# Two transformer blocks with product-key experts: expert picks in waves of 32 tokens, the convolution interleaved with the gathers

## The chip, the core and the metric

The program runs on one core of a Trainium2 chip, in fp32, for one sequence of 256 tokens of width 1024. The metric is the device time of one execution in microseconds. Before the change it is 2983.41 us, the median of 3 runs (2981.97 to 2993.83).

## The reference, cut to what matters

The first block has two layers. Each ends in an expert layer: per token and head, 16 experts of 16384 are chosen by product keys, and each chosen expert contributes one row of a table u (a dot product with the token) and one row of a table v (added with a weight). The mixer between the two expert layers is a convolution of 31 taps, so a token needs its neighbours 15 to either side. Then a second block of two layers (feed-forward, mixer, feed-forward) follows, which the change doesn't touch.

```python
s = jnp.einsum("thpd,hpnd->thpn", q, sub_keys)            # q = hb @ w_query, 8 heads, 2 halves
s_top, i_top = lax.top_k(s, 16)
cand = (s_top[:, :, 0, :, None] + s_top[:, :, 1, None, :]).reshape(...)
best, pos = lax.top_k(cand, 16)
expert = jnp.take_along_axis(cand_idx, pos, axis=-1)      # cand_idx = i_top[0] * 128 + i_top[1]
gate = jax.nn.softmax(best, axis=-1)
act = gelu(einsum("thkd,td->thk", jnp.take(u_tab, expert, axis=0), hb))
y = einsum("thk,thkd->td", gate * act, jnp.take(v_tab, expert, axis=0))
# a layer: h += g1 * mixer(modulate(rms_norm(h)));  h += g2 * experts(modulate(rms_norm(h)))
# mixer of layer 0: attention; of layer 1: conv = pw2(silu(layer_norm(depthwise31(glu(pw1(a))))))

```

## The kernel before

All five engines run programs written out in order; semaphores join them. Weights come as tiles of 512 KB (128 partitions of 1024 fp32 values), loaded by the sync engine SP in the order of the plan into four slots; SP refills a slot when TensorE (PE) has done with it. A tile is multiplied by `linear`: 8 matmuls, each recorded as two MATMUL rows, since an fp32 matmul leaves two records.

The phases are `ada`, `attn`, `peer` 0, `conv`, `peer` 1 and then the second block. An expert layer (`peer`) has 256 picks: head by head, for each of two blocks of 128 tokens, 16 picks. A pick `k` is one expert for each of 128 tokens:

- GpSimd (POOL) issues one indirect DMA (line 830) that fetches 128 rows of u and v together, 8 KB per token, 1.05 MB in all, into slot `k % PAIR_RING` of a ring of 14 slots. It waits until PE has used the slot's former content (`v_used`), and, every 16 picks, until VectorE (DVE) has chosen the experts (`expert_ready`).
- DVE makes the 128 dot products (line 2365), ScalarE (ACT) the gelu (1138), DVE multiplies by the gate (2372, `weigh`), ACT spreads the 128 weights on the diagonal of a 128x128 matrix (1145), and PE multiplies that by the rows of v in two matmuls of 512 columns (1742), which add up in two banks of PSUM per token block.

A choice (`choose`, lines 2309 to 2349) turns key scores of one head and 128 tokens into 16 experts. It stands on DVE two choices ahead of its use. Queries and scores of later heads are computed by PE between picks. The last four picks of a layer are summed by DVE. Then the sums are turned back, and the residual is updated for all tokens (`back`).

`conv` runs between the two expert layers, with no gather in flight: RMS norm, 16 tiles for `pw1` with a gate (ACT sigmoid 1188, DVE 2436), 31 taps per channel chunk (six chunks on DVE, line 2454; two on PE with diagonal matrices made by ACT, 1099), layer norm, `pw2`. The 14 last rows of the modulation weights (`rest_of_rows`, line 797) are loaded in it and reduced by DVE (2075). The first expert layer's `attn_w_out` product for the second token block runs inside `peer` 0 (`late`), as that of `pw2` does inside `peer` 1. After `peer` 1, `h_res` is turned to token-major (1793) and the feed-forward starts with row norms (ACT 922) and its first matmul (1679).

## Time and profile before

| | |
|---|---|
| median of 3 runs | 2983.41 us |
| span of the profiled execution | 2988.1 us |
| PE, DVE, ACT, POOL busy over the span | 87%, 65%, 37%, 21% |
| DMA | 832.42 MB, mean 279 GB/s |
| gathers (indirect DMAs) | 512 |
| weight tiles | 453 |

The profiled execution's own time is its span; nothing else of it is given. The page divides the span into 40 slices of 74.7 us. Its DMA row reads, in tenths of busy share and in GB/s:

```
DMA  9940899999999734999999998555425555542454
GB/s 299 391 163 1 300 419 420 420 420 420 421 420 420 304 99 140 420 417 420 420 420 420 420 420 355 183 183 168 156 67 183 183 161 184 183 161 75 150 188 148
```

So the 16 DMA engines are full in two long stretches, the expert layers, and nearly idle in the attention before them and in the convolution between them. "Busy" of an engine is the time in which an instruction of it is running; "idle before" names what ended a wait.

### The profile page before, as it was taken

The numbers are of one execution on the slowest core, as the hardware profiler recorded it, in microseconds if no ns is written. First come the engines' busy times: TensorE is split into PE (matmuls) and PEld (weight loads), VectorE is DVE, ScalarE is ACT, GpSimd is POOL, SyncE is SP. The second block draws the span as 40 slices with busy tenths as digits, with TensorE's granted clock in tenths as the row PEclk, the third lists the DMA queues.
The fourth block names the chain that finished last, engine by engine and source line by source line (L and its number), as shares of the span: only waits on it lengthen the run. The fifth ranks groups of instructions, "written<-read, shape, count | busy, mean of one in ns | idle before, by whom it ended". The sixth has DMA issues, their size and how long they took to land. (4 is left out here: it accounts for less than half of the span.)

```text
span 2988.1 us, 36198 instructions
## 1 busy us (share of the span) xinstructions
PE 2612.3 (87%) x11546; PEld 1723.9 (58%) x11546; DVE 1952.1 (65%) x4771; ACT 1112.4 (37%) x2639; POOL 633.9 (21%) x600
## 2 busy tenths in 40 slices
PE   7989888888777797898887787899989999999998
PEld 3534744333232387543333332898849989985798
DVE  1866476777676496686677765666746666675565
ACT  3245332222222312332222222445544454464544
POOL 0410245444444100354443542000000000000000
PEclk9989999999989898999999999899999999999999
DMA  9940899999999734999999998555425555542454
GB/s 299 391 163 1 300 419 420 420 420 420 421 420 420 304 99 140 420 417 420 420 420 420 420 420 355 183 183 168 156 67 183 183 161 184 183 161 75 150 188 148
DMA packets 152951, 832.42 MB, mean 279 GB/s; under 512 B 17008, under 2 KB 17136, under 8 KB 86384
## 3 DMA queue, kind: packets, MB, share of 16 engines
q0 software_dynamic: 85392, 579.38, 47.0%
q1 hardware_dynamic: 65664, 238.65, 24.1%
q10 hardware_dynamic: 1760, 12.70, 1.3%
q8 instruction: 71, 1.16, 0.2%
q14 instruction: 64, 0.52, 0.0%
HBM read 829.61 MB, written 1.05 MB: 278 GB/s over the span
## 5 line engine op out<-in xcount | busy, mean ns | idle before, releaser
L1742 PE MATMUL ps<-arena 128*128 128x512 f32 x1440 | 683.3, 619 | 162.4 <-ACT arena L1145 162.2
L2365 DVE SCALAR_TENSOR_TENSOR arena<-arena 128x1024 f32<-128x1024 f32 x368 | 450.1, 1224 | 227.4 <-DMA arena<-experts,arena 227.3
L1742 PEld LDWEIGHTS ps<-arena 128*128 128x128 f32 x1440 | 268.3, 195 | 562.8 <-ACT arena L1145 292.1
L830 POOL DMA_INDIRECT arena<-experts,arena x368 | 413.1, 1123 | 847.4 <-PE ps L1742 487.4
L2101 DVE TENSOR_TENSOR w_lo<-weights,w_hi 128x512 fp32r<-128x512 f32 x528 | 364.3, 691 | 280.7 <-ACT w_hi L910 278.8
L1145 ACT ACTIVATE arena<-con,arena 128x128 f32<-128x128 f32 x504 | 203.0, 403 | 730.1 <-DVE arena L2372 730.1
L910 ACT ACTIVATE w_hi<-weights 128x512 fp32r<-128x512 f32 x528 | 332.9, 632 | 375.4 <-PE ps L1681 278.8
L1679 PE MATMUL ps<-a_hi,w_hi 128*128 128x256 f32 x1408 | 399.8, 284 | 5.8 <-DVEq L2120 2.7
L1681 PE MATMUL ps<-a_hi,w_lo 128*128 128x256 f32 x1408 | 398.9, 283 | 0.0
L1680 PE MATMUL ps<-a_lo,w_hi 128*128 128x256 f32 x1408 | 398.9, 283 | 0.0
L1742 PE MATMUL ps<-held,arena 128*128 128x512 f32 x576 | 277.8, 625 | 79.6 <-ACT arena L1145 79.6
L1679 PEld LDWEIGHTS ps<-a_hi,w_hi 128*128 128x128 f32 x1408 | 270.5, 192 | 10.6 <-DVEq L2120 3.1
L1680 PEld LDWEIGHTS ps<-a_lo,w_hi 128*128 128x128 f32 x1408 | 270.5, 192 | 3.1
L1681 PEld LDWEIGHTS ps<-a_hi,w_lo 128*128 128x128 f32 x1408 | 270.4, 192 | 0.0
L1742 PEld LDWEIGHTS ps<-held,arena 128*128 128x128 f32 x576 | 109.8, 199 | 244.6 <-ACT arena L1145 131.9
L2365 DVE SCALAR_TENSOR_TENSOR held<-held,arena 128x1024 f32<-128x1024 f32 x144 | 175.9, 1222 | 83.5 <-DMA held<-experts,arena 83.5
L1435 PE MATMUL ps<-sq,weights 128*128 128x256 f32 (+1 forms) x1088 | 209.9, 355 | 17.9 <-ACT sq L904 12.3
L1435 PEld LDWEIGHTS ps<-sq,weights 128*128 128x128 f32 x1088 | 186.7, 201 | 44.3 <-issue 20.0
L830 POOL DMA_INDIRECT held<-experts,arena x144 | 163.8, 1138 | 199.1 <-PE ps L1742 184.4
L1011 ACT ACTIVATE arena<-ps 128x256 f32<-128x256 f32 (+5 forms) x182 | 83.4, 463 | 229.0 <-PE ps L1435 132.3
L1690 PE MATMUL ps<-w_hi,v_hi 128*128 128x512 f32 x352 | 138.6, 394 | 4.7 <-DVE v_lo L2521 4.7
L1690 PE MATMUL ps<-w_hi,v_lo 128*128 128x512 f32 x352 | 138.1, 392 | 0.0
(279 smaller groups left out, 3508.4 us busy)
## 6 DMA issues: line engine op xcount, KB each, us to landing
weights<-stream SPq DMA_DIRECT2D x453, 512.0 KB, 3.4
arena<-mod_rows_in POOLq DMA_DIRECT2D x71, 512.0 KB, 9.1
arena<-experts,arena POOLq DMA_INDIRECT x368, 25.8
mod_rows<-mod_rows_in POOLq DMA_DIRECT2D x9, 512.0 KB, 8.7
arena<-gain_rows ACTq DMA_DIRECT2D x1, 3072.0 KB, 11.5
held<-experts,arena POOLq DMA_INDIRECT x144, 26.1
arena<-rpb_windows ACTq DMA_DIRECT2D x4, 512.0 KB, 16.5
arena<-keys_in ACTq DMA_DIRECT2D x2, 1024.0 KB, 6.6
```

The source lines that it names most:

```text
L830: pool.indirect_dma_start(out=pair_of(k), out_offset=None, in_=experts[l], in_offset=bass.IndirectOffsetOnAxis(ap=expert[:, k:k + 1], axis ...
L910: act.activation(w_hi[:, o % 2, part], weights[:, t.unit, part], ACT.Copy).then_inc(hi_ready, 1)
L1011: taken(act.activation(dst, src, ACT.Copy), pr)
L1145: act.activation(diag[:, k % DIAGS, :], const("ident"), ACT.Copy, scale=act_w[:, k:k + 1]).then_inc(diag_ready, 1)
L1435: ins = pe.matmul(dst, wt(t, k, a, b), rhs(k), start=(k == 0), stop=(k == KC - 1))
L1679: pe.matmul(dst, w_hi[:, o % 2, cut], a_hi[:, k, :], start=(k == 0), stop=False)
L1680: pe.matmul(dst, w_hi[:, o % 2, cut], a_lo[:, k, :], start=False, stop=False)
L1681: ins = pe.matmul(dst, w_lo[:, o % 2, cut], a_hi[:, k, :], start=False, stop=(k == KC - 1))
L1690: ins = pe.matmul(ps[:, 2 * tb + half, :], v[:, b, at], w[:, o % 2, cut], start=(start and n == 0), stop=False, skip_group_check=True)
L1742: ins = pe.matmul(ps[:, 2 * b + half, :], diag[:, k % DIAGS, :], v_of(k, HALF * half, HALF * (half + 1)), start=(k == TOPK * b), stop=(k = ...
L2101: dve.tensor_tensor(w_lo[:, o % 2, part], weights[:, t.unit, part], w_hi[:, o % 2, part].bitcast(F32), ALU.subtract) \
L2365: dve.scalar_tensor_tensor(out=u, in0=u, scalar=1.0, in1=h_rows[:, b, :], op0=ALU.mult, op1=ALU.mult, accum_out=act_raw[:, k:k + 1]).then_ ...
```

## The change

The two expert layers and the convolution become one phase, `gather`, of 512 picks ("beats"). Every engine's program is generated from one table, `gather_order`: at each beat an engine does its part of pick `k` and then the steps that the table lists for it.

- A pick now serves 32 tokens and four heads (4 x 32 = 128 partitions) instead of 128 tokens and one head. Eight waves of 32 tokens per layer, two groups of heads per wave, 16 picks per group: 256 picks per layer, as before, and 32 choices in all, as before. Scores are computed per group, 32 rows at a time (`scores`), and the token rows are repeated four times (`rows`).
- A wave is finished after 32 picks. The diagonal matrix has 32 columns (`token`, 128x32), and the two matmuls of a pick write two of four column groups of the array (32 output partitions each, even picks groups 0 and 1, odd picks 2 and 3) in one bank. After each wave the sums are copied, added and turned by four small matmuls (`fold`), and DVE updates 32 columns of the residual in 8 operations.
- The gate is multiplied on ACT (a Copy with a scale) instead of on DVE. All 512 picks go through PE; the DVE sum of the last four is gone.
- The convolution runs in two blocks beside the gathers, block 0 from beat 130 and block 1 from beat 258: gates for 128 columns each, outputs for 96 and 160. Four channel chunks are tapped on PE (was two), four on DVE (was six). Queries of the second expert layer follow each block (96 and 160 columns), and `pw2` is whole per block.
- As each matrix is now used for two blocks of tokens, its tiles are loaded twice: 32 query tiles per layer (was 18), 32 for `pw1` (was 16), 16 for `pw2` (was 16 with the late half), 8 `late` tiles in layer 0: 120 tiles (was 76).
- The 14 modulation rows are loaded one by one between gathers of layer 0, into two slots.
- The ring of gathered pairs has 10 slots instead of 14 (`ARENA_PAIRS` 6 instead of 10, plus 4). The buffers of the convolution take the room.
- A choice stands on DVE at beat 16(c - 1) + 1, one group ahead; the first choice waits for the queries of four heads (8 tiles) where it waited for one head (2 tiles).

The core of the diff:

```diff
-PEER_BANKS = [4, 5, 6]
-TURN_BANK = 7
...
+FOLD_BANK, SCORE_BANK, TAP_BANK = 2, 3, 7
+WORK_BANKS = [4, 5, 6]
...
-TAPPED = [6, 7]
-EARLY_TAPS = 16
-ARENA_PAIRS = 10
...
+WAVE = 32
+WAVES = T // WAVE
+GROUP_HEADS = P // WAVE
+WAVE_GROUPS = H // GROUP_HEADS
+GROUPS = WAVES * WAVE_GROUPS
+WAVE_PICKS = WAVE_GROUPS * TOPK
+PICKS = GROUPS * TOPK
+GLU_COLS = [slice(0, 128), slice(128, 256)]
+OUT_COLS = [slice(0, 96), slice(96, 256)]
+WIDEST = 160
+PW1_ORDER = [4, 0, 1, 5, 2, 3, 6, 7]
+TAPPED = [4, 5, 6, 7]
+DIRECT = [(0, 1), (2, 3)]
+TAP_PART = 4
+TAP_DIAGS = 8
+ARENA_PAIRS = 6
 PAIR_RING = ARENA_PAIRS + 4
-TAP_ROWS = 8
...
+    for m in range(2 * H):
+        put("query", 0, 0, m, pe=-1, act=-1)
+        if m % (2 * GROUP_HEADS) == 2 * GROUP_HEADS - 1:
+            c = m // (2 * GROUP_HEADS)
+            put("scores", c, pe=-1, act=-1)
+            put("choose", c, dve=c - 1)
+            if c == 0:
+                put("rows", 0, pe=-1, act=-1)
...
+    for m in range(KC):
+        put("late", m, pe=1 + m, dve=6 + 5 * (m // 4))
+    put("late_squares", 0, act=12)
+    put("late_norm", 0, pe=13, act=14, dve=15)
+    put("shift_late", 0, act=16)
+    for m in range(2 * H):
+        put("query", 0, 1, m, pe=20 + 4 * m, act=21 + 4 * m)
+    for k in range(LATE_ROWS):
+        put("late_row", k, pool=16 + 6 * k, dve=20 + 6 * k)
...
+    for b, base in enumerate((130, 258)):
+        put("conv_squares", b, act=base + 1)
+        put("conv_sum", b, pe=base + 2, act=base + 3, dve=base + 4)
+        put("conv_shift", b, act=base + 5)
+        for i, c in enumerate(PW1_ORDER):
+            put("pw1", b, c, pe=base + 6 + 3 * i, act=base + 8 + 3 * i, dve=base + 9 + 3 * i)
+        for n, pair in enumerate(DIRECT):
+            first = base + (16, 25)[n]
+            for part in range(0, TAPS, TAP_PART):
+                put("direct", b, n, part, dve=first + part // TAP_PART)
+        parts = -(-TAPS // TAP_PART)
+        for n, c in enumerate(TAPPED):
+            for part in range(parts):
+                beat = base + 11 + parts * n + part
+                put("diags", b, c, part, act=beat)
+                put("taps", b, c, part, pe=beat + 1)
+            put("tap_out", b, c, act=base + 11 + parts * (n + 1) + 1)
+        last = base + 12 + parts * len(TAPPED)
+        put("mean", b, pe=last + 1, dve=last + 2)
+        put("var", b, act=last + 3, pe=last + 4)
+        put("var_root", b, act=last + 5)
+        put("spread", b, dve=last + 6, act=last + 7)
+        for m in range(KC):
+            put("pw2", b, m, pe=last + 8 + m, dve=last + 10 + m)
+        put("next_squares", b, act=last + 19)
+        put("next_sum", b, pe=last + 20, act=last + 21, dve=last + 22)
+        put("next_shift", b, act=last + 23)
+        for m in range(2 * H):
+            beat = last + 24 + (2 * m if b == 0 else m if m < H else m + 2)
+            put("query", 1, b, m, pe=beat, act=beat + 1)
+    put("new_keys", 0, act=222)
+    for c in range(2, ALL_GROUPS):
+        beat = TOPK * (c - 1)
+        late = 3 if c == GROUPS + WAVE_GROUPS * 3 else 0
+        put("scores", c, pe=beat - 6 + late, act=beat - 4 + late)
+        put("choose", c, dve=beat + 1)
+        put("exps", c, act=beat + 6)
+    for v in range(ALL_WAVES):
+        if v:
+            put("rows", v, pe=WAVE_PICKS * v - 12, act=WAVE_PICKS * v - 10)
+        end = WAVE_PICKS * (v + 1)
+        put("fold", v, act=end, pe=end + 1, dve=end + 2)
+    return order
+
+
+ORDER = gather_order()
+FIRST_BEAT, END_BEAT = -1, ALL_PICKS + 3
+TILED_STEPS = {"query": 1, "pw1": 2, "pw2": 1}
+
...
+            def late_row(k):
+                pool.wait_ge(row_dot, EARLY_ROWS if k < 2 else EARLY_ROWS + k - 1)
+                pool.dma_start(late_slots[k % 2], mod_rows_in[EARLY_ROWS + k]).then_inc(late_landed[k % 2], 16)
...
-                        pool.wait_ge(expert_ready, CHOICES * l + k // TOPK + 1)
-                    if base + k >= PAIR_RING:
-                        pool.wait_ge(v_used, base + k - PAIR_RING + 1)
-                    if l == 0 and k == LATE_SLOT:
-                        last = PL["peer", l]["t_late"][KC - 1]
-                        pool.wait_ge(tile_done[last.unit], last.first)
+                        pool.wait_ge(expert_ready, k // TOPK + 1)
+                    if k >= PAIR_RING:
+                        pool.wait_ge(v_used, k - PAIR_RING + 1)
...
+                    act.wait_ge(dot_done, k + 1)
+                    act.activation(act_out[:, one], act_raw[:, one], ACT.Gelu).then_inc(gelu_done, 1)
+                    if k % TOPK == 0:
+                        act.wait_ge(gate_set, k // TOPK + 1)
+                    act.wait_ge(gelu_done, k + 1)
+                    act.activation(act_w[:, one], act_out[:, one], ACT.Copy, scale=gate[:, one]).then_inc(weighed, 1)
+                    act.wait_ge(weighed, k + 1)
+                    if k >= DIAGS:
+                        act.wait_ge(v_used, k - DIAGS + 1)
+                    act.activation(diag[:, k % DIAGS, :], const("token"), ACT.Copy, scale=act_w[:, one]) \
+                        .then_inc(diag_ready, 1)
...
+                    pe.wait_ge(diag_ready, k + 1)
+                    pe.wait_ge(pair_landed[k % PAIR_RING], landed(k))
+                    for half in range(2):
+                        first = WAVE * (2 * (k % 2) + half)
+                        ins = pe.matmul(ps[first:first + WAVE, v % 2, :], diag[:, k % DIAGS, :],
+                                        v_of(k, HALF * half, HALF * (half + 1)), start=(k % WAVE_PICKS < 2),
+                                        stop=(k % WAVE_PICKS >= WAVE_PICKS - 2), skip_group_check=True)
+                    ins.then_inc(v_used, 1)
...
+                        for h in range(GROUP_HEADS):
+                            m = 2 * (first + h) + e
+                            ins = pe.matmul(bank(pr)[WAVE * h:WAVE * (h + 1), NKEY * e:NKEY * (e + 1)],
+                                            pq[:, m, WAVE * wave:WAVE * (wave + 1)], sub_keys[:, m, :],
+                                            start=True, stop=True, skip_group_check=True)
...
+                def fold(v):
+                    pr = pl["fold", v]
+                    pe.wait_ge(y_copied, v + 1)
...
+                    for c in range(4):
+                        ins = pe.matmul(bank(pr)[:, 2 * WAVE * c:2 * WAVE * (c + 1)], y_wave[:, P * c:P * (c + 1)],
+                                        const("halves"), start=True, stop=True)
...
+                    if k % WAVE_PICKS == 0:
+                        wait_taken(dve, pl["rows", v][1])
+                    u = u_of(k)
+                    dve.wait_ge(pair_landed[k % PAIR_RING], landed(k))
+                    dve.scalar_tensor_tensor(out=u, in0=u, scalar=1.0, in1=h_rows[:, v % 2, :], op0=ALU.mult,
+                                             op1=ALU.mult, accum_out=act_raw[:, at:at + 1]).then_inc(dot_done, 1)
```

## Rows read from the trace of the kernel before

**Rows 1.** Busy time by stretch; columns on the first row.
```profile
core 0: us, PE busy (x) PEld busy (x) DVE busy (x) ACT busy (x) POOL busy (x), PEclk, DMA share, GB/s
340.00:1010.00 670.00, 544.56 (x1373) 249.83 (x1371) 464.85 (x1379) 189.39 (x612) 285.75 (x254) 0.95 1.01 416
1013.00:1187.00 174.00, 142.31 (x709) 125.42 (x710) 127.93 (x320) 46.89 (x117) 7.39 (x14) 0.86 0.40 134
```

**Rows 2.** Timeline: one pick in the steady state.
```profile
1846.34 1.23 DVE L2365 SCALAR_TENSOR_TENSOR held<-held,arena 128x1024 f32<-128x1024 f32 x1 [1.17 <-DMA held<-experts,arena]
1847.68 0.40 ACT L1145 ACTIVATE arena<-con,arena 128x128 f32<-128x128 f32 x1 [1.98 <-DVE arena L2372]
1847.98 0.19 ACT L1138 ACTIVATE arena<-arena 128x1 f32<-128x1 f32 x1
1848.13 1.99 PE L1742 MATMUL ps<-arena 128*128 128x512 f32 x4 [0.49 <-ACT arena L1145]
1848.82 1.22 DVE L2365 SCALAR_TENSOR_TENSOR held<-held,arena 128x1024 f32<-128x1024 f32 x1 [1.17 <-DMA held<-experts,arena]
```

**Rows 3.** Timeline: first gather of each expert layer.
```profile
337.58 1.01 POOL L830 DMA_INDIRECT arena<-experts,arena  x1 [165.55 <-DVE arena L2349]
...
1187.82 0.99 POOL L830 DMA_INDIRECT arena<-experts,arena  x1 [161.70 <-DVE arena L2349]
```

**Rows 4.** Timeline: last dot product of each expert layer.
```profile
1012.90 1.23 DVE L2365 SCALAR_TENSOR_TENSOR arena<-arena 128x1024 f32<-128x1024 f32 x1 [0.16 <-DMA arena<-experts,arena]
...
1863.91 1.23 DVE L2365 SCALAR_TENSOR_TENSOR arena<-arena 128x1024 f32<-128x1024 f32 x1
```

**Rows 5.** DMA queues from 337 to 1013 us: packets, MB, share.
```profile
q0 software_dynamic: 36864, 268.45, 95.7%
q1 hardware_dynamic: 3080, 11.18, 4.2%
```

**Rows 6.** Windows: one near the end of a layer, one after a POOL pause.
```profile
1009.00:1010.00 1.00, 0.00 (x0) 0.00 (x0) 0.93 (x3) 0.03 (x1) 0.00 (x0) 1.00 0.06 25
1280.00:1282.00 2.00, 2.00 (x6) 0.94 (x5) 2.00 (x4) 0.80 (x4) 1.64 (x1) 1.00 1.04 360
```

**Rows 7.** Timeline: start of the feed-forward stage.
```profile
1875.67 1.02 ACT L922 ACTIVATE sq<-ps 128x1024 f32<-128x1024 f32 x1 [6.86 <-PE ps L1793]
1885.17 0.58 PE L1679 MATMUL ps<-a_hi,w_hi 128*128 128x256 f32 x1 [2.71 <-DVEq L2120]
```

**Rows 8.** Timeline: a weight tile, first choice.
```profile
307.41 1.95 PE L1435 MATMUL ps<-arena,weights 128*128 128x128 f32 x16
...
328.01 0.49 DVE L2309 MAX8 arena<-arena 128x8 f32<-128x128 f32 x2 [4.28 <-ACT arena L1011]
...
337.13 0.18 DVE L2349 SCALAR_TENSOR_TENSOR arena<-arena 128x16 uint32<-128x16 f32 x1
```

**Rows 9.** Timeline: convolution taps, tap diagonals, and narrower vector work.
```profile
346.01 2.19 DVE L2172 SCALAR_TENSOR_TENSOR sq<-h_res,gain,rstd 128x128 f32<-128x128 f32 x8 [2.13 <-ACT rstd L896]
...
1042.65 2.44 ACT L1099 ACTIVATE arena<-con,cols 128x128 f32<-128x128 f32 x8
1050.98 9.59 DVE L2454 SCALAR_TENSOR_TENSOR arena<-arena,cols 128x256 f32<-128x256 f32 x24
```

**Rows 10.** Groups of instructions, ACT, 337 to 1013 us: table loads.
```profile
L1138 ACT ACT_TABLE_LOAD x16 | 20.5, 1283 | 0.3
```

**Rows 11.** Timeline: 32-column matmuls of the first stage, PE.
```profile
30.11 1.92 PE L1469 MATMUL ps<-weights,cond 128*32 128x512 f32 x16
39.85 1.05 PE L1469 MATMUL ps<-weights,cond 128*32 128x512 f32 x4 [0.19 <-DMA weights<-stream]
```

**Rows 12.** Timeline at the end of that pause: POOL, thirty gathers issued before.
```profile
1277.95 1.35 POOL L830 DMA_INDIRECT arena<-experts,arena  x1 [9.97 <-PE ps L1742]
```

**Rows 13.** DMA queues from 1187 to 1278 us.
```profile
q0 software_dynamic: 4221, 30.80, 81.8%
```

**Rows 14.** Issues on the page: count, median us to landing.
```profile
arena<-experts,arena POOLq DMA_INDIRECT x368, 25.8
```

966 lines of the change are left out of this document (463 added, 503 removed).

## Prediction, made before the change was run

> **What bounds the kernel now.** I read the page's slices first, then the windows of two stretches, then the timeline around the two expert layers, then the DMA queues of one layer. In [rows 1] the first expert layer (the second is alike) runs at a DMA share of 1.01 and 416 GB/s, while DVE is busy 465 of 670 us, PE 545, ACT 189: the 16 DMA engines set the pace and no compute engine is full. Between the two lies a stretch of 174 us with 134 GB/s, in which PE (142 us) and DVE (128 us) do the convolution one after the other. A steady pick shows the same thing closely: dots start 2.48 us apart (1846.34, 1848.82), each waits some 1.17 us for its gather, and the matmuls of a pick take 1.99 us of that period [rows 2].
>
> From the first gather to the last dot layer 0 takes 1012.90 - 337.58 = 675.3 us, layer 1 676.1 us [rows 3, 4]. In layer 0's time the queues moved 268.45 + 11.18 = 279.6 MB, with 0.4 MB of instruction fetch 280.0 MB [rows 5]. The steady rate is 420.5 GB/s (the page's full slices say 420 and 421), which makes 665.9 us; 9.4 us remain for start and drain. The drain has a row: at 1009 us the share is 0.06, that is one engine of 16 still working while 15 have ended [rows 6]. I use: stage = bytes / 420.5 GB/s + 9.5 us.
>
> **The change part by part.** The profiled execution's own time is its span, 2988.1 us, 4.7 us above the median of the three runs (2983.4). All terms are made against the span. Fixed points are the first gather at 337.6 us and the first feed-forward matmul at 1885.2 us [rows 3, 7]: 1547.6 us lie between them. What is ahead and behind is untouched.
>
> *Start.* The first choice waits for 8 query tiles instead of 2: 6 x 1.95 us = 11.7 us [rows 8]. Key scores of four heads are 16 records instead of 4; at the tile's 1.95 / 16 = 0.12 us that is 1.5 us more, and nothing more if four column groups overlap (below). I take 0.9, as the operands arrive late for part of it. The choice itself (328.0 to 337.3 us, 9.3 us, [rows 8]) has the same operations on 128 partitions. First gather at 337.6 + 12.6 = 350.2 us. The turned rows (`rows` 0) and the other 8 query tiles lie beside the choice.
>
> *The stage.* Gathers: 512 x 1.0486 = 536.9 MB, unchanged. Tiles: 120 instead of 76 for the phase; about 15 have been loaded before the first gather (11 used, 4 slots), 4 for the feed-forward are loaded at the end: 109 x 0.524 = 57.1 MB. The 14 modulation rows move among the gathers: 7.3 MB. Keys of layer 1: 1.0 MB. Instruction fetch 0.8 MB. Sum 603.2 MB, at 420.5 GB/s 1434.4 us, + 9.5 = 1443.9 us. So 44 more tiles cost 44 x 1.25 = 55 us of DMA time, and the gap of 1187.8 - 1012.9 = 175 us is what pays for them. One drain instead of two saves some 9 us, inside this sum.
>
> *Does something else hold the stage up?* The work is summed by engine against the 1444 us.
> DVE: dots 512 x 1.22 = 625; 32 choices x 9.3 = 298 and 0.6 each for the gate sums, 19; taps, where a 256-column one costs 9.59 / 24 = 0.40 us [rows 9] and a 128-column operation 2.19 / 8 = 0.27, hence some 0.24 at 96 and 0.30 at 160 columns: 124 x 0.24 + 124 x 0.30 = 67; norms, gates, layer norm, `pw2`, folds, modulation rows about 90. Sum 1100 us, 76%. `weigh` goes (0.15 us and a wait each).
> ACT: per pick gelu 0.19, the gate 0.19, the narrow diagonal between 0.19 and 0.40, with gaps 0.75 us: 384; 248 tap diagonals x 0.31 (2.44 / 8) = 76; table loads of 1.28 us [rows 10]: 64 for the exps as now, 32 for the 16 sigmoids, some 20 others: 149; copies and shifts 100. Sum 710 us, 49%.
> PE: in the first stage 16 records of 512 columns on 32-column groups took 1.92 us, 4 alone 1.05 us, where the 4 of a pick on the full array take 1.99 [rows 2, 11]. The lower end of a pick is thus 0.48, the upper 1.05 us if two groups overlap; I take 1.05, as a pick stands alone: 538 us. Tiles 120 x about 2 = 240; taps 67, scores and turned rows 60 to 180, sums 30. About 1000 us, 70%, against 545 of 670 us in a layer now.
> So no engine is full on average. POOL has 512 issues of about 1.25 us, 640 us.
>
> *The order within the stage.* A step that waits holds its engine's later picks. The ring decides how long the DMA engines go on: 10 slots. A pick takes from landing to release a dot (1.22), ACT 0.75, PE 1.05, POOL 1: 4 us, 2 slots, so 8 gathers, 20 us, are queued. How far may this fall? POOL paused 9.97 us until 1277.95, with 30 gathers of the layer issued [rows 12]; the queue had by 1278 us moved 30.80 MB, 29.4 gathers [rows 13], and still the next window shows only a dip, to 360 GB/s [rows 6]. So the queue may fall to nearly nothing if the 16 engines are even; if one is 9 us behind, as in the drain [rows 6], 11 us of cover are left.
> A choice holds DVE 9.9 us; one idle gap of 1.2 covers part: 8.7 us. Below 11, so 0 us. (A choice at 16(c-1)+1 ends 8 beats before POOL can ask for its experts, since the ring allows only 9 ahead.)
> Direct taps are the tight place. Block 1, beats 273 to 290 (18 beats): dots 22.0, two choices 18.6, taps 37, six gates 3, a fold 1.7: 82.5 us. DMA needs 18 x 2.485 + 10 tiles x 1.25 = 57 us. Short by 25 us, with 11 to 20 us of cover: loses 5 to 14 us. Block 0 the same with 96 columns: short by 17 us, loses 0 to 6. Waits of DVE for PE or ACT in the norm and layer-norm chains, spread one beat apart by the table, hit its 24% of slack: 0 to 10. I take 14 us of all this.
>
> *POOL's late rows* wait for DVE's use of the row two back; POOL reaches beat 16+6k when DVE is at 7+6k, and the wait is for 8+6k: one beat, nothing.
>
> *The end.* Now from the last dot (1863.9) to the first feed-forward matmul 21.3 us [rows 4, 7]. After: dot 1.3, gelu, gate, diagonal 0.8, PE 1.05, copy 0.6 with gaps 0.9, fold 0.7, eight small DVE operations 1.6, while the first half of `h_res` is turned already: ACT's row squares start 6.4 us after the dot, and from there to the matmul it is 1885.2 - 1875.7 = 9.5 us [rows 7]. 15.9 us.
>
> *Sum.* 12.6 + 1443.9 + 14 + 15.9 = 1486.4, against 1547.6: 61.2 us less. 2988.1 - 61.2 = 2926.9 by the span, 2983.4 - 61.2 = 2922.2 by the median.
>
> *A rule against it.* A pick on 32-column groups is followed at each beat by full-array work. [rows 2, 11] show isolated bursts in either form, and not the one right behind the other in a dense stretch.
> The Trainium skill (TensorEngine Tiling (Array Packing), Key Properties) says that changing the tiling mode drains TensorE. By that rule every pick would stand alone twice over.
> A mechanism of this kernel that has that effect is priced from rows in rival 2.
> For ACT, the rows show a table load of 1.28 us with the next operation right behind.
> The Trainium skill (ScalarE: Activation LUTs, What ACT_TABLE_LOAD costs) adds a drain of 1380 ns to each switch; as an estimate by that page ACT would have 116 x 1.38 = 160 us more, 60% busy. The trace of before doesn't show the drain.
>
> **The rivals.**
> 1. *The ring of ten is too short.* Now a gather takes 25.8 us from issue to landing [rows 14], 10.4 of the 14 slots at 2.48 us each, so 3.6 slots are in release. With 3.6 of 10, 6.4 gathers (15.9 us) are queued, and with the 9 us of one late engine 6.9 us of cover remain. Then each of 32 choices loses 8.7 - 6.9 = 1.8 us, 58 us, and the taps 18 + 10 us: 86 instead of 14 us, 2922 + 72 = 2994 us. Half of it is 2958 us. For: the ring falls from 14 to 10 while DVE's holds stay. Against: the release is shorter by PE's 0.9 us and the DVE gate, and full rate was seen with an almost empty queue.
> 2. *Slower: the column groups don't overlap in this use.* Then a pick costs PE 1.99 us as now [rows 2]: 512 x 1.99 = 1019, with the other 460 to 520 (scores and rows at their upper end) 1500 us. At the granted clock of 0.95 of full [rows 1] that is 1580 us; PE starts at 322 and ends at 1902 with no wait at all, and waits some 40 us more for choices and chains (it idles 125 of 670 us now, most of it for DMA), so 1942, then 12 us to the feed-forward: 69 us later than now, 3052 us. It decides from about 1.8 us per pick on (PE then needs what DMA needs). For: two groups instead of four, mixed with full-array work. Against: 4 records in 1.05 us, alone [rows 11].
> 3. *ACT or the ping-pong of steps binds in the blocks.* From beat base+11 to base+29 ACT has 0.75 + 4 x 0.31 + 2.9 / 3 + 0.2 = 3.2 us a beat against 3.3 of DMA. If each of its waits and table loads costs half as much again, 1.4 us x 19 beats x 2 blocks = 53 us, less the cover of 11 each: 31 us. Chains of eight handoffs per block at 2 us not hidden: 32 us. Together 2922 + 63 - 14 = 2971 us at worst, 2945 in the middle.
> 4. *The convolution isn't hidden*: block 0 isn't ready for the choice at beat 241 and the gathers stop. All is one order, so this can only come out as 1 or 3; a stop of 50 us would give 2972.
>
> **How the numbers follow.** Forecast (DMA-bound, 0 to 30 us lost): 60%, 2905 to 2940. Rival 1 12% (2940 to 2994), rival 3 15% (2935 to 2971), rival 4 5%, rival 2 5%, and 3% that tiles cost less than priced, under 2905. A measurement of this kernel tells 0.5%, 15 us, from no change, so faster ends at 2968: 88% faster, 5% same, 7% slower. The range reaches from 2900 (nothing lost, 2908, and a rate of 422 GB/s, 5 us less, and a cheaper start) to 2962.
>
> **What the profile would show.** One stretch from 350 to about 1795 us with a DMA share near 1.01; first gather at 350 us; last dot at 1796 to 1825; first feed-forward matmul near 1824; 512 + 120 loads in it. Dips in GB/s, if any, near beats 155 and 285 (around 780 and 1150 us). PE's pick takes 1.05 us, not 1.99. Dips of 2 us every 40 us, under each choice, are rival 1; a DMA share below 0.95 with PE full is rival 2; ACT full in the two blocks is rival 3. The forecast is wrong if the mean rate in the stage is below 412 GB/s or the bytes are not 603 MB.

## The result, and the profile after

The changed kernel takes 3032.2 us (median of four runs, 3030.9 to 3039.6) against 2988.5 us for the kernel before beside it (2982.0 to 2993.8): the ratio is 1.015, 95% interval 1.013 to 1.0173. It is 1.5% slower, where 2% faster was forecast (2922 us, made against 2983.4, the median of three of these four runs). The profiled execution has a span of 3031.3 us, 43.2 us more than the 2988.1 of before.

The slices of the page of after: busy tenths of PE, DVE and ACT, the granted clock, the DMA share and GB/s, 75.8 us each.

```profile
PE   7989765655777766767855555899999999998998
...
DVE  1866357576664666676577776566746666675565
ACT  3245243333664435654444443445635454464544
...
PEclk9989887866878877988977677799999999999999
DMA  9940899999978999888999999555425555552454
GB/s 313 375 153 1 293 418 419 418 420 420 352 273 330 400 419 419 329 316 310 398 420 420 421 420 421 213 184 177 157 70 174 186 159 185 184 163 80 148 184 151
```

The two expert layers are one stretch now, as forecast, and most of it runs at the steady rate. But it has two holes, slices 11 to 13 and 17 to 19. They are the two blocks in which convolution work lies beside the gathers, and the windows size them (busy time by stretch; the columns are those of [rows 1]):

```profile
350.00:780.00 430.00, 268.55 (x1528) 111.49 (x1527) 279.18 (x728) 170.72 (x534) 178.89 (x163) 0.75 1.01 416
780.00:1050.00 270.00, 207.99 (x1356) 127.73 (x1354) 173.32 (x522) 149.73 (x434) 92.73 (x76) 0.84 0.88 333
1050.00:1220.00 170.00, 107.58 (x597) 48.69 (x594) 101.11 (x262) 71.92 (x220) 61.13 (x56) 0.77 1.01 419
1220.00:1440.00 220.00, 158.27 (x993) 97.92 (x991) 152.76 (x441) 123.01 (x345) 68.27 (x55) 0.89 0.83 315
1440.00:1910.00 470.00, 292.71 (x1508) 90.75 (x1508) 312.14 (x797) 192.27 (x628) 191.65 (x177) 0.75 1.00 415
```

At 333 GB/s for 270 us the first block falls behind a rate of 420.5 by 270 x (1 - 333/420.5) = 56 us, the second at 315 GB/s for 220 us by 55 us: 111 us. Outside the blocks the rate is 415 to 419. And over a block no engine is full: PE has 77%, DVE 64%, ACT 55% in the first, and 72%, 69% and 56% in the second. So the engines seem to wait for one another there. The stage behind is that of before: 3031.3 - 1930.3 = 1101.0 us from its first matmul, against 2988.1 - 1885.2 = 1102.9 ([rows 7]).

The start, the end and the bytes, from two timelines and the DMA queues between 350 and 1915 us:

```profile
349.82 1.01 POOL L899 DMA_INDIRECT arena<-experts,arena  x1 [177.02 <-DVE arena L2458]
...
1913.11 1.23 DVE L2477 SCALAR_TENSOR_TENSOR arena<-arena 128x1024 f32<-128x1024 f32 x1 [1.25 <-DMA arena<-experts,arena]
...
1930.34 0.58 PE L1783 MATMUL ps<-a_hi,w_hi 128*128 128x256 f32 x1 [2.72 <-DVEq L2248]
```

```profile
DMA packets 91798, 604.07 MB, mean 386 GB/s; under 512 B 10192, under 2 KB 10192, under 8 KB 26035
```

From first gather to last dot it is 1563.3 us; 604.07 MB at 420.5 GB/s and 9.5 us make 1446.1. The stretch is 117 us too long, and the two blocks hold 111 of them. ("Shortfall" below is this sum over the two windows: what DMA would have needed less at 420.5 GB/s.)

The waits of the first block (780 to 1050 us): who waited for whom, us in total, times, longest.

```profile
POOL arena L899 <- PE ps L1831: 101.6, 38, 9.0
...
PE ps L1831 <- ACT arena L1185: 56.1, 24, 8.9
DVE arena L2531 <- ACT arena L1250: 36.0, 6, 9.4
ACT arena L1177 <- DVE held L2477: 32.6, 10, 8.3
ACT arena L1177 <- DVE arena L2477: 26.9, 8, 8.3
...
ACT arena L1262 <- PE ps L1916: 22.0, 8, 5.2
DVE arena L2579 <- PE ps L1539: 18.7, 8, 6.3
ACT arena L1084 <- PE ps L1539: 16.8, 8, 2.3
...
DVE arena L2561 <- PE ps L1545: 13.6, 1, 13.6
...
DVE arena L2477 <- DMA arena<-experts,arena: 9.2, 4, 3.1
...
DVE held L2477 <- DMA held<-experts,arena: 7.8, 5, 2.3
```

Each engine waits for others. POOL (the gathers, L899) waits for PE's picks (L1831); these for ACT's narrow diagonals (L1185); ACT's Gelu (L1177) for DVE's dots (L2477); DVE's gate (L2531) for ACT's sigmoid (L1250); ACT's tap diagonals (L1262) for PE's taps (L1916). DVE waits for DMA, which it does at every pick of the steady state ([rows 2]), only 9 times for 17 us here. The timeline shows how the waits hang together, in 13 us of the first block:

```profile
849.03 4.88 PE L1539 MATMUL ps<-sq,weights 128*128 128x128 f32 x32
...
850.61 1.22 DVE L2477 SCALAR_TENSOR_TENSOR held<-held,arena 128x1024 f32<-128x1024 f32 x1
...
853.75 1.03 PE L1916 MATMUL ps<-arena 128*128 128x96 f32 x8
854.15 1.28 ACT L1262 ACTIVATE arena<-con,cols 128x128 f32<-128x128 f32 x4 [4.77 <-PE ps L1916]
...
855.19 1.03 PE L1831 MATMUL ps<-arena 128*32 128x512 f32 x4
...
856.15 1.13 PE L1916 MATMUL ps<-arena 128*128 128x96 f32 x8
856.22 1.28 ACT L1250 ACT_TABLE_LOAD   x1
856.50 0.94 POOL L899 DMA_INDIRECT arena<-experts,arena  x1 [6.14 <-PE ps L1831]
857.21 1.05 PE L1831 MATMUL ps<-held,arena 128*32 128x512 f32 x4
857.52 0.37 ACT L1250 ACTIVATE arena<-ps,cols 128x128 f32<-128x128 f32 x1
...
857.92 0.35 DVE L2531 SCALAR_TENSOR_TENSOR arena<-ps,cols,arena 128x128 f32<-128x128 f32 x1 [6.09 <-ACT arena L1250]
...
859.04 1.28 ACT L1177 ACT_TABLE_LOAD   x1
860.26 1.22 DVE L2477 SCALAR_TENSOR_TENSOR held<-held,arena 128x1024 f32<-128x1024 f32 x1
```

Read it from the top. PE works off the two tiles of one chunk of the first convolution, 4.88 us in one go. ACT meanwhile wants to write tap diagonals, finds the ring of eight full, and waits 4.77 us for PE's taps, which stand behind those tiles. Only then come its pick, a table load and the sigmoid. DVE, which wants to gate, has waited 6.09 us for that sigmoid, and its next dot starts at 860.26, 9.65 us after the one at 850.61. POOL had no slot to fill for 6.14 us. Next time round PE is the one that waits: its pick at 861.27 us sat 1.95 us for the diagonal of that late dot.

The deepest hole, in the second block, has one engine full for a while:

```profile
1310.00:1320.00 10.00, 5.68 (x18) 2.77 (x19) 9.86 (x29) 4.19 (x16) 1.95 (x1) 0.66 0.13 34
```

```profile
1313.38 0.20 ACT L1177 ACTIVATE arena<-arena 128x1 f32<-128x1 f32 x1 [9.36 <-DVE arena L2477]
...
1314.32 1.92 PE L1831 MATMUL ps<-arena 128*32 128x512 f32 x4 [6.80 <-ACT arena L1185]
...
1316.53 1.95 POOL L899 DMA_INDIRECT arena<-experts,arena  x1 [9.90 <-PE ps L1831]
```

From 1300.97 to 1312.12 us DVE works off a part of its taps and then a choice of experts, and starts no dot. ACT, PE and POOL wait in turn for the next one, and DMA moves 34 GB/s for 10 us. Cut into 49 windows of 10 us, the two blocks have ten in which DVE is busy 9.4 us or more, and these hold 32 of the 111 us. So "no engine is full" holds for the blocks and for 30 us (at most 27 us of 30 where the rate is below 350 GB/s), but not for 10 us.

### The profile page after: what moved, and what is told of

Read it like the earlier page. It is cut to its first block and busy times, and to the rows that moved or that the text cites. A ratio compares the mean times of both kernels' runs of the same rounds, so it can differ in the third digit from the quotient of the medians.

```text
span 3031.3 us, 42342 instructions
## 1 busy us (share of the span) xinstructions
PE 2421.9 (80%) x14174; PEld 1576.2 (52%) x14174; DVE 1897.2 (63%) x4413; ACT 1402.2 (46%) x3482; POOL 641.6 (21%) x600
## 3 DMA queue, kind: packets, MB, share of 16 engines
HBM read 852.73 MB, written 1.05 MB: 282 GB/s over the span
## 5 line engine op out<-in xcount | busy, mean ns | idle before, releaser
L1831 PE MATMUL ps<-arena 128*32 128x512 f32 x1232 | 390.9, 776 | 321.8 <-ACT arena L1185 311.2
L899 POOL DMA_INDIRECT arena<-experts,arena x308 | 347.9, 1129 | 723.3 <-PE ps L1831 519.9
L2477 DVE SCALAR_TENSOR_TENSOR arena<-arena 128x1024 f32<-128x1024 f32 x308 | 370.9, 1225 | 201.1 <-DMA arena<-experts,arena 198.7
L1831 PE MATMUL ps<-held,arena 128*32 128x512 f32 x816 | 265.5, 779 | 201.4 <-ACT arena L1185 192.2
L1177 ACT ACTIVATE arena<-arena 128x1 f32<-128x1 f32 x512 | 101.7, 199 | 627.9 <-DVE arena L2477 368.7
L1831 PEld LDWEIGHTS ps<-arena 128*32 128x32 f32 x1232 | 51.3, 121 | 537.2 <-ACT arena L1185 505.5
L2477 DVE SCALAR_TENSOR_TENSOR held<-held,arena 128x1024 f32<-128x1024 f32 x204 | 246.2, 1223 | 128.9 <-DMA held<-experts,arena 127.8
L899 POOL DMA_INDIRECT held<-experts,arena x204 | 236.9, 1161 | 378.0 <-PE ps L1831 360.6
L1539 PE MATMUL ps<-sq,weights 128*128 128x128 f32 (+2 forms) x1792 | 262.1, 308 | 3.6 <-ACT sq L973 1.8
L1084 ACT ACTIVATE arena<-ps 128x512 f32<-128x512 f32 (+6 forms) x248 | 103.1, 423 | 257.9 <-PE ps L1539 169.9
L1831 PEld LDWEIGHTS ps<-held,arena 128*32 128x32 f32 x816 | 34.0, 121 | 347.7 <-ACT arena L1185 325.7
L1185 ACT ACTIVATE arena<-con,arena 128x32 f32<-128x32 f32 x512 | 165.2, 323 | 16.8
L1181 ACT ACTIVATE arena<-arena 128x1 f32<-128x1 f32 x512 | 150.8, 295 | 23.1 <-DVE arena L2468 6.7
```

The lines of the kernel that those rows point to most:

```text
L899: pool.indirect_dma_start(out=pair_of(k), out_offset=None, in_=experts[k // PICKS], in_offset=bass.IndirectOffsetOnAxis(ap=expert[:, at:at ...
L1084: taken(act.activation(dst, src, ACT.Copy), pr)
L1181: act.activation(act_w[:, one], act_out[:, one], ACT.Copy, scale=gate[:, one]).then_inc(weighed, 1)
L1185: act.activation(diag[:, k % DIAGS, :], const("token"), ACT.Copy, scale=act_w[:, one]) \
L1539: ins = pe.matmul(dst, wt(t, k, a, b), rhs(k), start=(k == 0), stop=(k == KC - 1))
L1831: ins = pe.matmul(ps[first:first + WAVE, v % 2, :], diag[:, k % DIAGS, :], v_of(k, HALF * half, HALF * (half + 1)), start=(k % WAVE_PICKS ...
```

## The experiments

Theory A, from these rows: the engines form a loop. Each works strictly in order, each step is handed on one or two beats later, so a stop on one is passed round, and time is lost though no engine is full over the block. Its rivals: B, ACT's own work and its table loads; C, the ring of ten gathered pages; D, PE's work; and later E, DVE's work. The first four kernels each change one of these.

**Sixteen tap diagonals instead of eight.** The second buffer for the late modulation rows shares their room.

```
-TAP_DIAGS = 8
+TAP_DIAGS = 16
...
-late_slots = [mod_flat[:, D:2 * D], R["row"]]
+late_slots = [mod_flat[:, D:2 * D], R["taps"][:, 0:D]]
```

> The ring of tap diagonals holds 16 instead of 8 (the second late-row buffer shares their room). After the change loses about 120 us of DMA time, 59 in each convolution block, none outside. Theory A (lock-step: ACT can't make the diagonals of part n before PE has used those of part n - 2, so ACT waits behind PE's two pw1 tiles and PE then waits for ACT): ACT's 22 us of waiting for PE's taps in the window 780 to 1050 us goes, and the time falls by 25 to 50 us to about 2990. Theory B (ACT has too much to do, above all table loads): no change, within 5 us. Theory C (the gather ring of 10 is too short for DVE's holds): no change, within 5 us. Theory D (PE has too much to do in the blocks: 11.4 us per three beats): at most 10 us less.

Measured 3013.3 us, ratio 1.0078 (1.0042 to 1.0115). The same work with a longer ring is some 20 us shorter. That is less than the 25 to 50 us that theory A was given, and more than B (within 5 us) and D (at most 10) allow: a sum of work alone doesn't explain it.

**The sigmoids' table loads away.** Gelu stands in for the sigmoid of the gate, so that ACT doesn't switch sets.

```
-ACT.Sigmoid, bias=col("b_pw1", 8 + c)
+ACT.Gelu, bias=col("b_pw1", 8 + c)
```

> The gate's sigmoid is a gelu here (another function, so the output differs), which leaves the activation table in place: 32 table loads of 1.28 us, 41 us of ACT, are gone, all in the blocks. Theory B (ACT's work and loads): 30 to 40 us less. Theory A (lock-step with the tap diagonals): 5 to 15 us less, since ACT's answer to PE comes 1.3 to 2.6 us sooner once in three beats. Theory C (gather ring): 0 to 5 us less. Theory D (PE's work): 0 to 5 us less.

Measured 3001.7 us, ratio 1.0050 (1.0037 to 1.0063): 30 us less. Between 350 us and the last dot 30 loads of 1.28 us are gone, 38.5 us. This is what theory B was expected to give (30 to 40 us), and twice the 5 to 15 us of theory A. So some three quarters of ACT's loads come back as time, though ACT is busy 55% over the block: they seem to stand where others wait for it. B by itself is ruled out by the run before and by the spaced tiles below, in which ACT's work is the same and the time isn't.

**Fewer taps on PE and ACT.** Of the 31 taps of each of their four chunks, 4 are made.

```
+PT = 4
...
-put("diags", b, c, part, act=beat)
-put("taps", b, c, part, pe=beat + 1)
+if part == 0:
+    put("diags", b, c, part, act=beat)
+    put("taps", b, c, part, pe=beat + 1)
```

> Of the 31 taps that PE makes for each of four channel chunks per block only the first 4 are left (27 of 31 left out, with their diagonals on ACT, so the output differs); every other step stays at its beat. PE has 216 x 0.28 = 60 us less work, ACT 216 x 0.31 = 67 us. Theory A (lock-step): 50 to 80 us less, the gate waits on DVE shrink. Theory D (PE's work): 40 to 60 us less. Theory B: 30 to 50 us less. Theory C (gather ring): 0 to 15 us less.

Measured 2962.4 us, ratio 0.9917 (0.9889 to 0.9944), 70 us below after, and faster than before, though it leaves work out. Only theory A's range (50 to 80 us) holds it; D had 40 to 60, B 30 to 50. Its blocks run at 395 and 374 GB/s. Even this much work away doesn't fill the holes wholly: 270 x (1 - 395/420.5) + 220 x (1 - 374/420.5) = 41 us stay.

**Ring of eight gathered pages instead of ten.**

```
-ARENA_PAIRS = 6
+ARENA_PAIRS = 4
```

> The ring of gathered pairs has 8 slots instead of 10. Theory C (ring too short, rival 1 of the prediction): the holds of DVE under 32 choices then cost 2 to 5 us each more, 60 to 150 us slower, with dips of the DMA rate outside the blocks too. Theories A, B and D: the blocks lose the cover of two gathers each time they fill again, 10 to 30 us slower, and outside the blocks the rate stays at 418 to 421 GB/s.

Measured 3043.7 us, ratio 1.0182 (1.0135 to 1.0230). That is some 10 us more, from two runs, and the interval overlaps that of after. Theory C's 60 to 150 us are out. The shortfall of the two blocks hardly grows (113 against 111 us). Most of the rest lies just ahead of the second window, where that block's first tiles stand: 408 GB/s between 1050 and 1220 us against 419, with 300 from 1200 to 1210. The window from 350 to 780 us of this kernel:

```profile
350.00:780.00 430.00, 269.18 (x1534) 112.87 (x1532) 281.03 (x732) 173.35 (x539) 173.25 (x161) 0.75 1.01 414
```

414 GB/s with eight, 416 with ten, with the choices of that stretch in both: C falls as the cause of 117 us. More than ten slots, as before had, wasn't tried, since there is no room for them.

**First-convolution tiles spaced.** The same work, other beats.

```
-PW1_ORDER = [4, 0, 1, 5, 2, 3, 6, 7]
+PW1_ORDER = [4, 5, 0, 1, 6, 2, 3, 7]
+PW1_AT = [6, 10, 14, 18, 22, 26, 29, 32]
...
-put("pw1", b, c, pe=base + 6 + 3 * i, act=base + 8 + 3 * i, dve=base + 9 + 3 * i)
+put("pw1", b, c, pe=base + PW1_AT[i], act=base + PW1_AT[i] + 2, dve=base + PW1_AT[i] + 3)
...
-first = base + (16, 25)[n]
+first = base + (22, 33)[n]
```

> Same work, other beats: the pairs of first-convolution tiles stand at beats 6, 10, 14, 18, 22, 26, 29, 32 of their block instead of every third beat from 6 to 27, the chunks in the order 4, 5, 0, 1, 6, 2, 3, 7, and the vector engine's taps begin at beats 22 and 33 instead of 16 and 25. Theory A (the engines wait for one another in a loop, and a beat in which TensorE works off a pair of tiles, 4.9 us, together with picks and taps stops the others): 8 pairs that stood three beats apart cost about (13.7 - 9.8) = 3.9 us per three beats, some 31 us a block; spread over four beats a third of it goes: 3032 - 20 = 3012 (3000 to 3025). Theory B (ScalarE's work sets it) and D (TensorE's work sets it): the sum of neither changes, so 3032 +- 5.

Measured 3003.4 us, ratio 1.0057 (1.0040 to 1.0074): 29 us less. Theory A had said 20 less (7 to 32), B and D nothing. This is the plainest sign that the order, and not a sum over the block, sets the time: not an instruction is added or removed. The edit moves three things, the tiles, the order of the chunks and the start of DVE's taps; which of them brings how much wasn't separated.

**Two chunks to DVE.**

```
-TAPPED = [4, 5, 6, 7]
-DIRECT = [(0, 1), (2, 3)]
+TAPPED = [6, 7]
+DIRECT = [(0, 1), (2, 3), (4, 5)]
...
-first = base + (16, 25)[n]
+first = base + (16, 25, 33)[n]
...
-beat = base + 11 + parts * n + part
+beat = base + 27 + parts * n + part
...
```

> Chunks 4 and 5 of the depthwise convolution go from TensorE (and their diagonals from ScalarE) to VectorE: in both blocks together 124 tap products of 0.15 to 0.18 us off TensorE, 124 diagonals of 0.32 us off ScalarE (40 us), and 124 multiply-adds of 0.24 (block 0) and 0.31 us (block 1), 34 us, onto VectorE. If the pair of ScalarE and TensorE sets the pace (theories A, B, D), the run with 216 taps left out gained 70 us, 0.32 us each, so 124 give 40 us: 2992 (2980 to 3002). Theory E (VectorE, the third in the loop, is as near its end): the 34 us added there eat most of it, in block 1 above all, where a beat with eight of its 160-column taps holds 2.5 + 1.3 us against 3.3: 3015 to 3035, with block 0 better and block 1 no better than in the kernel after.

Measured 2987.6 us, ratio 0.9998 (0.9988 to 1.0008), 45 us less than after, though 34 us of work went onto DVE: the largest gain of a single edit that keeps the function. A, B and D had all said 40 (2980 to 3002), so it doesn't tell them apart; E's 3015 to 3035 is out. The blocks run at 378 and 334 GB/s against 333 and 315, so the second, with its wider taps, gained less. And DVE is now full for 30 us at a time in both blocks, with the rate still low in the second:

```profile
840.00:870.00 30.00, 19.38 (x95) 10.55 (x93) 29.46 (x111) 15.44 (x51) 7.82 (x7) 0.77 0.95 369
...
1250.00:1280.00 30.00, 16.54 (x78) 9.25 (x78) 29.48 (x102) 12.53 (x42) 9.87 (x6) 0.83 0.73 276
```

**Tanh for the sigmoid, and sixteen diagonals.** The gate is the same function: 0.5 + 0.5 tanh(x/2), one DVE instruction more per chunk; the bias column is halved once.

```
-TAP_DIAGS = 8
+TAP_DIAGS = 16
...
-ACT.Sigmoid, bias=col("b_pw1", 8 + c)
+ACT.Tanh, scale=0.5, bias=col("b_pw1", 8 + c)
...
+link(dve.tensor_scalar(s, s, 0.5, 0.5, ALU.mult, ALU.add))
```

> The same function as the kernel after: the sigmoid of the gate is made as 0.5 + 0.5 tanh(x/2), with tanh from a table set that also holds the Gelu of the picks, if the compiler's sets allow it, for one more VectorE instruction per chunk (16 of some 0.2 us); and the ring of tap diagonals has 16 instead of 8. The two parts alone gave 30 us (there another function stood in for the sigmoid) and 19 us. Theory A: both shorten the one loop and add up in part: 3032 - 45 = 2987 (2978 to 2997). Theory B (ScalarE's work alone): the loads go, the ring does nothing more: 3002.

Measured 2996.7 us, ratio 1.0028 (1.0014 to 1.0042). Tanh needs no load of its own beside Gelu: between 350 us and the last dot L1177 has 41 loads instead of 55, and L1250 none instead of 16. The two parts give 36 us together where they gave 19 and 30 singly, at the upper edge of the time that theory A allowed (2978 to 2997), and 5 us below B's 3002. With the loads gone, the longer ring adds little.

**Both, and the tiles spaced.**

> The tanh and 16 diagonals of the run before and the spaced pairs of tiles together. Theory A: 2987 - 15 = 2972 (2960 to 2985), at last below the kernel before. Theories B and D: spacing adds nothing, the same time as the run without it within 5 us.

Measured 2977.5 us, ratio 0.9962 (0.9950 to 0.9974): below the kernel before, and in theory A's range (2960 to 2985); B and D had said that spacing adds nothing to the run before, and it adds 19 us. DVE fills up here too; three windows in its first block:

```profile
800.00:830.00 30.00, 25.69 (x209) 17.46 (x209) 16.22 (x50) 19.86 (x65) 9.38 (x8) 0.89 1.00 398
830.00:860.00 30.00, 28.52 (x212) 20.02 (x211) 29.04 (x106) 17.13 (x62) 10.60 (x10) 1.00 1.00 400
860.00:890.00 30.00, 25.56 (x160) 14.45 (x158) 29.00 (x89) 22.91 (x77) 16.59 (x10) 0.94 0.95 352
```

The same windows of after read:

```profile
800.00:830.00 30.00, 24.36 (x198) 17.74 (x196) 25.60 (x86) 16.95 (x47) 7.26 (x6) 0.89 0.84 311
830.00:860.00 30.00, 23.68 (x152) 16.56 (x152) 14.76 (x48) 19.46 (x51) 6.33 (x7) 0.83 0.79 276
860.00:890.00 30.00, 20.42 (x102) 12.05 (x102) 24.86 (x97) 16.11 (x48) 5.76 (x5) 0.75 0.75 267
```

In the last two, DVE has 29 of 30 us where it had 15 and 25. With the waits shortened, one engine's sum begins to count.

**All four together.** Tanh, 16 diagonals, spaced tiles, two chunks on DVE. PE's taps come three a beat instead of four, their diagonals stand two beats ahead instead of one, and DVE's taps have other beats.

```
+PW1_ORDER = [0, 1, 6, 2, 3, 7, 4, 5]
+PE_PART = 3
+TAPPED_AT = [18, 30]
+DIRECT_AT = [[14, 17, 18, 19, 20, 22, 23, 24], [25, 26, 27, 28, 29, 33, 34, 35], range(36, 44)]
...
```

> Tanh, 16 diagonals, spaced pairs of tiles, and chunks 4 and 5 on VectorE in one kernel: TensorE's tap products of chunks 6 and 7 come three a beat from beats 18 and 30 of a block, their diagonals two beats ahead instead of one, and VectorE's taps lie on beats 14 to 43 but for the two or three after an expert choice. Theory A (one loop of waits through all engines; what shortens or loosens it anywhere counts, until the beat of 3.3 us is met): moving the two chunks gave 44 us by itself, tanh and 16 diagonals 36 of the 49 us they gave singly, spacing 19 of 29; so about 60% of the 44 comes on top of 2977: 2951 (2940 to 2962). If VectorE, which the move loads with 34 us, is now what the blocks wait for: 2970 to 2980.

Measured 2980.1 us, ratio 0.9975 (0.9966 to 0.9985): a miss of 29 us against theory A's 2951. What was worth 45 us alone is worth nothing on top of the others. The second case that the expectation named holds (DVE is what the blocks wait for, 2970 to 2980), and the windows show DVE at its end in both blocks:

```profile
830.00:860.00 30.00, 24.92 (x160) 16.52 (x158) 28.86 (x108) 15.15 (x53) 7.53 (x8) 0.89 1.01 409
...
1240.00:1270.00 30.00, 20.67 (x112) 12.51 (x110) 29.11 (x99) 15.98 (x50) 7.80 (x7) 0.89 0.89 331
...
1300.00:1330.00 30.00, 11.60 (x102) 6.22 (x104) 20.29 (x61) 15.00 (x34) 6.75 (x6) 0.73 0.68 241
```

The last row is another kind of hole, 241 GB/s with PE at 39%: the layer norm, whose steps go PE, DVE, ACT, PE, ACT, DVE, ACT, PE on beats one apart.

**The steps behind the taps of block 0 two beats apart.** Block 1 has no idle beats for it.

```
-put("mean", b, pe=last + 1, dve=last + 2)
-put("var", b, act=last + 3, pe=last + 4)
+t = [1, 2, 3, 4, 5, 6, 7] if b else [2, 4, 6, 8, 10, 12, 13]
+put("mean", b, pe=last + t[0], dve=last + t[1])
+put("var", b, act=last + t[2], pe=last + t[3])
...
```

> The kernel of the run before, with the steps that follow the taps of block 0 (mean, variance, root, spread, second convolution, next norm, queries) two beats apart instead of one, where the order has some twenty idle beats before the scores need the queries; block 1 is unchanged. In the stretch from 900 to 940 us of the tanh and spaced run the gathers ran at 278 and 303 GB/s against 420, a loss of 12 us. Theory A: most of these come back: 8 to 12 us below the run before, 2941. If the single sums of work set it: the same time.

Measured 2968.2 us, ratio 0.9942 (0.9923 to 0.9961), 10 to 12 us less, by the ratios or the medians (8 to 12 expected). Block 0 goes from 383 to 404 GB/s, block 1 stays (344 and 345).

**Few taps on DVE**, the counterpart of the third run, on the kernel after.

```
-for part in range(0, TAPS, TAP_PART):
+for part in range(0, TAP_PART, TAP_PART):
```

> The kernel after with 27 of the 31 taps of each of VectorE's four chunks left out in both blocks (the depthwise sums of those chunks are cut short): 216 multiply-adds of 0.24 and 0.31 us, 59 us of VectorE, and nothing of ScalarE or TensorE. It is the counterpart of the run that left out 216 taps of the other two engines and gained 70 us. Theory A with VectorE as a full member of the loop: 0.5 to 0.8 us of time for each us taken away: 3032 - 40 = 2992 (2980 to 3003). If only ScalarE and TensorE hold each other up, and VectorE's taps lie in its waits: 3025 to 3032.

Measured 3018.8 us, ratio 1.0104 (1.0087 to 1.0121). 59 us of DVE's work are worth 13 us. Both expectations missed: theory A with DVE as a full member had 2980 to 3003, PE and ACT alone 3025 to 3032. Taking 27 of 31 taps from PE and ACT brought 70 us, taking them from DVE 13. So the time of the kernel after hangs above all on PE and ACT, and most of DVE's taps seem to lie in DVE's own waits; how much of the rest its choices cost (the hole at 1310 us) no run shows. In the kernels in which DVE fills up, it is a limit behind the first one.

**The best order.** Tanh, 16 diagonals, spaced tiles, and the steps of block 0 two beats apart.

> Tanh, 16 diagonals and spaced pairs (2977), with the steps behind the taps of block 0 two beats apart: they gave 12 us in the run that had chunks 4 and 5 on VectorE too. Theory A: 2977 - 12 = 2965 (2958 to 2971), and with the chunks on VectorE no better (2968 there), since VectorE is busy 29 of 30 us in the blocks in either. If the gain of 12 us hung on the moved chunks: 2977.

Measured 2964.9 us, ratio 0.9920 (0.9907 to 0.9932), as theory A had it (2958 to 2971): 0.8% faster than before, 67 us less than after. Its two blocks:

```profile
780.00:1050.00 270.00, 211.00 (x1442) 123.91 (x1436) 203.85 (x609) 147.77 (x474) 114.04 (x92) 0.89 1.00 406
1220.00:1440.00 220.00, 172.81 (x1096) 106.98 (x1094) 150.68 (x417) 103.28 (x318) 75.80 (x61) 0.91 0.92 356
```

All runs in one table: the gain on after, worked out as (1.0151 - ratio) x 2988 us, beside the shortfall of the two blocks against 420.5 GB/s, worked out as above from the profiled execution. (A gain can differ by 1 or 2 us from the difference of the medians given above, since each ratio has its own runs of before.)

| kernel | ratio to before | gain on after, us | GB/s in the blocks | shortfall, us |
|---|---|---|---|---|
| after | 1.0151 | | 333, 315 | 111 |
| ring of eight pages | 1.0182 | -9 | 332, 313 | 113 |
| few taps on DVE | 1.0104 | 14 | 341, 320 | 104 |
| 16 diagonals | 1.0078 | 22 | 351, 321 | 97 |
| tiles spaced | 1.0057 | 28 | 360, 334 | 84 |
| sigmoid loads away | 1.0050 | 30 | 362, 331 | 84 |
| tanh, 16 diagonals | 1.0028 | 37 | 367, 332 | 81 |
| two chunks to DVE | 0.9998 | 46 | 378, 334 | 73 |
| all four | 0.9975 | 53 | 383, 344 | 64 |
| tanh, 16, spaced | 0.9962 | 56 | 380, 348 | 64 |
| all four, steps apart | 0.9942 | 62 | 404, 345 | 50 |
| few taps on PE and ACT | 0.9917 | 70 | 395, 374 | 41 |
| best order | 0.9920 | 69 | 406, 356 | 43 |

Gain and shortfall add up to 104 to 120 us in every row: nearly all of the time is lost in the two blocks, and what an edit brings it brings there.

What the runs show and what they don't: that the loss lies in the blocks, and that it changes with the beats and with a ring while the work stays the same, is shown. That it is passed round as one loop is read from the two timelines, and theory A's range held the result in eight of the twelve runs: it gave the table loads too little, and too much to the ring of diagonals, to DVE's taps and to the two chunks on top of the rest.

## Why the prediction was wrong

*Right.* The bound outside the blocks (416 to 419 GB/s, DMA share 1.01). The first gather, 349.8 us against 350.2. The bytes, 604.1 MB against 603.2. The end from the last dot to the feed-forward, 17.2 us against 15.9. The place of the first dip, near 780 us; the second was put near 1150 and comes about 80 us later. Two of the engines' sums: PE 1000 us forecast, ACT 710; the windows from 350 to 1931 us add up to 1049 and 722. DVE was put at 1100 and has 1029. So the balance of the whole stage was right to some 7%, and it didn't matter. The sign that the prediction named for its own failure is there: a mean rate below 412 GB/s, 386 as measured.

*The step that failed* is "The order within the stage", and in it the sentences "Waits of DVE for PE or ACT in the norm and layer-norm chains, spread one beat apart by the table, hit its 24% of slack: 0 to 10. I take 14 us of all this." The measured loss is 117 us. The waits that made it are not those of DVE in the norm chains alone: PE's picks waited for ACT's diagonals, ACT for PE's taps and for DVE's dots, and DVE's gates for ACT's sigmoids, and of these waits the sum had nothing. With this one term put right, 1486.4 + 103 = 1589.4 us stand for the 1547.6 of before, which makes 3029.9 us by the span, and 3031.3 was measured; so the other terms together were right to 2 us. The part for DVE's taps, 5 to 20 us for the two blocks, fits the 13 us that leaving most of them out gave.

What was wrong with the step is its form. It summed each engine's work against the beats and asked how much of a queue covers a hold. That holds for one engine that stops by itself on a full queue, such as a choice outside the blocks; there the forecast of 0 us was right, since the rate is 415 to 419 GB/s. In the blocks it wasn't: the choice at 1303 us met a queue that was already short, and DMA moved 34 GB/s behind it. It doesn't hold where engines hand work round. DVE's slack of 24% (36% in the block as measured) is no cover when DVE's next step waits for ACT, ACT's for PE's taps, and PE's taps stand behind tiles of 4.88 us. The slack is then just the name of those waits.

*Rival 3* named the mechanism, "ACT or the ping-pong of steps", and mis-sized it: 31 us for ACT and 32 us for the chains, 2971 us at worst, with 15%. Its sign, ACT full in the blocks, isn't there (55%); the ping-pong is. ACT's beat of 3.2 us against 3.3 was close to what the trace has, and was a warning: an engine at 97% of the beat has no room for any wait. In the timeline above three picks (855.19, 857.21, 861.27 us on PE) take the 13 us in which DMA, at 3.3 us a beat, could bring four. The rival took the cover of the gather queue off each block once, 11 us; a loss that recurs for forty beats isn't covered by a queue that has no time to fill again. Both its parts are borne out: the chains by the 12 us that spreading the steps of one block gave, ACT by the 30 us of the table loads. The ring of diagonals, 20 us, and the other beats of tiles and taps, 28 us, are parts that it lacked.

*Rival 1* (2994 us): refuted as a loss at each choice, by the steady rate with ten and with eight pages. *Rival 2* (3052 us): the right sign for another reason. A pick takes PE 1.03 to 1.05 us in the dense stretch at full clock, as forecast, so the column groups do overlap, right behind full-array work too.
The rule of the Trainium skill that speaks against this (TensorEngine Tiling (Array Packing), Key Properties: a change of tiling mode drains TensorE) shows no cost here: the pick at 857.21 us, with no gap behind eight full-array records, takes 1.05 us like the one that stands alone in [rows 11].
The other rule of the Trainium skill, the drain of 1380 ns beside each table load (ScalarE: Activation LUTs, What ACT_TABLE_LOAD costs), isn't seen either: the load at 856.22 us starts 0.02 us behind ACT's instruction before it, ends at 857.50, and the sigmoid starts at 857.52.
*Rival 4*: no stop; from the second gather on no gather waited for a choice. *POOL's late rows*, put at nothing, did wait for DVE, seven times for 25 us, but the rate of that stretch stayed at 416 GB/s.

*The range* of 2900 to 2962 added rivals as if only one term could go wrong by its own bound. The term had a bound of 30 us at best guess, though the trace of before shows no stretch with five kinds of work handed between engines beat by beat. A bound for it would have had to ask what happens when the engines work one after the other.

*Left open.* Of the 117 us, 6 aren't in the two blocks' windows. The best order still falls short by 43 us, 34 of them in block 1, where the layer norm's steps are one beat apart and no idle beats are left. Whether PE's picks one or two beats behind ACT's would mend it wasn't tried. How much of PE's 208 us in the block is owed to its granted clock of 0.84 wasn't separated either: of the 4.88 us of the two tiles at 849 us, the first 2 us (849 to 851) ran at a granted clock of 0.50, while a tile alone took 1.95 us in [rows 8]. A slower PE is thus part of what goes round, and no run holds the order still and changes the clock.

## What to carry to other kernels

Before work of one stage is laid among the steps of another, draw the loop: for each added step, which engine's next step waits for it, and what stands in front of it in that engine's order; sum the waits round the loop for the densest few beats, not each engine's work over the stage. Look for the longest piece that stands in front of a hidden step: here two tiles of 4.88 us and a choice of 9 us against a beat of 3.3. Longer lags and longer rings helped (10 to 12 us for steps two beats apart, 20 us for 16 diagonals); that a lag must exceed the longest piece is a guess that no run here tests.

When no engine is full and the pace is still lost, moving steps to other beats is free and brought 29 us. Moving work between engines paid as well, 45 us, before any engine was full over 30 us. But the gains don't add up: once DVE was busy 29 of 30 us, the same move was worth nothing. So look after each step for the engine that has filled up.
